# Stick-breaking attention: masking by a product on TensorE, or by a scan that restarts and a multiplication on GpSimd

## The chip, the cores and the metric

The kernel runs on one core of one Trainium2 chip. The time is the device time of one execution in microseconds, the median of three runs. One launch computes the whole model; everything happens on one core, so that one slow stage shows in the time directly.

The core's engines: TensorE (PE in the profile, PEld its weight loads), VectorE (DVE), ScalarE (ACT), GpSimd (POOL), and SyncE (SP), which here only issues the DMAs.

## The reference, cut to what matters

The model has 512 tokens of width 1024 and runs a first block (chunked attention and convolution), then two layers with an MLP each. The mixer of the last layer is "stick-breaking" attention with 8 heads of 128. That part is what the change touches:

```python
def blk_fn(args):
    i, qb = args
    z = jnp.einsum('bthd,bshd->bhts', qb, k).astype(jnp.float32) * d_h ** -0.5
    t_pos = i * SB_QBLOCK + jnp.arange(SB_QBLOCK)
    mask = key_pos[None, :] < t_pos[:, None]
    lo = jnp.where(mask, jax.nn.log_sigmoid(-z), 0.0)
    rc = lax.cumsum(lo, axis=3, reverse=True)
    log_a = jax.nn.log_sigmoid(z) + (rc - lo)
    a = jnp.where(mask, jnp.exp(log_a), 0.0)
    return jnp.einsum('bhts,bshd->bthd', a.astype(v.dtype), v)
```

For each query the softplus of the scores is summed from the last valid key backwards; a weight is exp(score minus that sum). A key counts only if it stands before the query, so in each diagonal block of 128 x 128 only the strict lower triangle is valid.

## The kernel before, in words

The program of each engine is written out by hand, with semaphores between them; nothing reorders it. Activations stand with channels on the partitions. A weight tile of 1024 x 256 (`raw`, 1 MB) is loaded by SP, rounded by ACT (`split`, line 1068, `wh<-raw`), and the rest is taken by DVE (`split`, line 1724, `wl<-raw,wh`, 128 x 2048); PE then makes three products per block (lines 451 to 453).

The last mixer is the stage `stick`: four groups of two heads (`attention_group`, g = 0 to 3), numbered 12 to 19, and a fifth call that only finishes heads 18 and 19 beside the first part of the output projection. In group g PE projects the six blocks of its own two heads (q, k, q, k, and values twice) and, between them, works off the two heads of the group before. Its program in groups 1 to 3 is: scores of the even head (`do_scores(0)`); blocks 0 and 1; the sum of squares of block 0 (`head_stat`); transposes of the even head's weights (`do_turns(0)`, line 555); block 2; `head_stat`; the product with the values of the even head (line 891); scores of the odd head; block 3; `head_stat`; block 4; transposes of the odd head (`do_turns(1)`); block 5; `head_stat`; the values' product of the odd head.

Scores of one head are a lower triangle by row blocks of 128 queries: 128, 256, 384 and 512 columns, in three PSUM banks. Behind each score product stands a second one, of an identity with a 128 x 128 mask of 0 and -1e30, which is added onto the diagonal block (lines 538 and 541).

The weights then come about in two halves (`HALVES`): the row blocks 0 to 2 (768 columns), and row block 3 (512 columns). ACT makes the softplus (`softplus`, lines 1380, 1383, 1384), DVE adds max(score, 0) (line 2263), scans backwards (line 2268, `suffix`, once per row block; the factor of the scan is `extra`, all ones), and subtracts the scan from the score in PSUM (line 2273), ACT takes the exponential (line 1393) and raises `a_ready`. The scan starts at the last column of a row block. A masked score of -1e30 has a softplus of 0 and a weight of exp(-1e30) = 0, so the masked columns change nothing.

PE's transposes are 10 blocks of 128 x 128: the first three wait for the first half (and for the PSUM banks, which DVE's line 2273 frees), the fourth for the second half. So one head's weights go round ACT, DVE, ACT before PE may go on, and PE stands still if they are late.

On DVE the odd head's last line 2273 is followed at once by `split(st, 2)`, one instruction of line 1724. GpSimd squares the q and k blocks for the norm (line 1693, and the low part, line 1698), and in the finishing call it splits one tile (line 1708); it has nothing to do with the weights. On ACT the exponentials stand in a fixed place between the evacuations of blocks.

Of the kernel before, what the change touches and what calls it, by code (L numbers as in the profile page):

```python
# [20 lines left out]
P = 128  # L21
# [104 lines left out]
def build(nc, xT, wst, par_d, wg_d, rb_d, small_d, mask_d, tab_d, tok_d, gain_d, out):  # L126
    with ExitStack() as ctx:
        def sb(name, shape, dt=F):
            return ctx.enter_context(nc.sbuf_tensor(name, shape, dt))
# [26 lines left out]
        ones_r = sb("ones_r", [P, P], R)  # L156
        ident_r = sb("ident_r", [P, P], R)
        mask_r = sb("mask_r", [P, P], R)
        SbB = sb("SbB", [P, 1280])
# [54 lines left out]
        g_log, g_scan, g_exp, g_prod, g_silu = (sem(n) for n in ("g_log", "g_scan", "g_exp", "g_prod", "g_silu"))  # L214
        sp_log, a_ready = sem("sp_log"), sem("a_ready")
        ob_lo = sem("ob_lo")
# [152 lines left out]
        def _(sp):  # L369
# [47 lines left out]
            ready(sp, ("gout", 1, 1))  # L417
            sp.dma_start(small[:, C_SN:C_SN + P], mask_d).then_inc(tables_in, 16)
            with sp.Fori(GLA_END, N_TILES // 2) as i:
# [8 lines left out]
        def _(pe):  # L428
# [101 lines left out]
            def scores(hd, q, k, rows):  # L530


                before = hd >= 12
                for b in range(3):
                    take(("score", hd, b))
                for t in range(NT):
                    w, b = (t + 1) * P, MIX[side(hd)][CBANK[t]]
                    last = mm(ps[b][:, COFF[t]:COFF[t] + w], q[rows, t * P:(t + 1) * P],  # L538
                              k[rows, 0:w], start=True, stop=not before)
                    if before:  # L540
                        last = mm(ps[b][:, COFF[t] + t * P:COFF[t] + w], ident_r[:], mask_r[:],
                                  start=False, stop=True)
                    if t:
                        last.then_inc(done[b], 1)
# [512 lines left out]
        def _(act):  # L1057
# [300 lines left out]
            def attention_group(name, g, hd, prev, qk0, soft):  # L1358
# [27 lines left out]
                def exponential(hh, *halves):  # L1386

                    if not soft:
                        for banks in halves or HALVES:
                            b, lo, w = banks[-1]  # L1390
                            settled(act, ("score", hh, b))
                            x = MIX_Sb[side(hh)][:, banks[0][1]:lo + w]
                            A(x, x, ACT.Exp).then_inc(a_ready, 1)

# [161 lines left out]
        def _(pool):  # L1556
# [130 lines left out]
            mlp("ffn0", 0, 4)  # L1687

            for n in range(16):
                st, q = Step("stick", n // 4), SQ[("qk", 8 + n)]  # L1690
                whole, (hi, lo) = sq[:, q % 2, :], sq_parts[n % 2]
                stands(pool, st, n % 4)
                g.tensor_tensor(whole, tmp[:, n % 2, :], tmp[:, n % 2, :], ALU.mult).then_inc(sq_whole, 1)
                pool.wait_ge(sq_whole, n + 1)
                pool.wait_ge(sq_ready, q + 1)
                if n >= 2:
                    pool.wait_ge(sq_used, STAT[("qk", 8 + n)] - 1)
                g.tensor_tensor(lo, whole, hi.bitcast(F), ALU.subtract).then_inc(sq_low, 1)


            so_ = Step("outc", 0)
            s = so_.slot(1)
            for a, ready_ in enumerate((third_hi, w_hi)):
                pool.wait_ge(ready_, so_.tile(1) + 1 if a else 1)
                if a:
                    pool.wait_ge(w_lo, so_.tile(1))
                for c in range(a * KC // 2, (a + 1) * KC // 2):
                    ins = g.tensor_tensor(wl[s][:, c, :], raw[s][:, c, :], wh[s][:, c, :].bitcast(F), ALU.subtract)
                ins.then_inc(w_lo if a else third_lo, 1)
            out_squares("outc", 5)  # L1710
            mlp("ffn1", 32, None)
# [3 lines left out]
        def _(dve):  # L1715
# [483 lines left out]
            def attention_group(name, g, hd, prev, qk0, soft):  # L2199
# [42 lines left out]
                def weights(hh, whole=True, last=None):  # L2242
# [17 lines left out]
                    for n, banks in enumerate(HALVES):  # L2260
# [5 lines left out]
                        for t in (3,) if n else (0, 1, 2):  # L2266
                            back = slice(OFF[t], OFF[t] + (t + 1) * P)
                            last = v.tensor_tensor_scan(suffix[:, back][:, ::-1], extra[:, 0:(t + 1) * P],  # L2268
                                                        Sb[:, back][:, ::-1], 0.0, ALU.mult, ALU.add)
# [84 lines left out]
            def mlp(name, hid0, key, n):  # L2354
# [22 lines left out]
                if not hid0:  # L2377
                    dve.wait_ge(tables_in, 48)
                    step(v.tensor_copy(ident_r[:], ident))
                    step(v.tensor_copy(ones_r[:], ones[:]))  # L2380
                    v.tensor_copy(mask_r[:], small[:, C_SN:C_SN + P]).then_inc(masks_set, 1)
                with dve.Fori(1, 3) as i:
# [3 lines left out]
            mlp("ffn0", 0, ("norm", 3), 4)  # L2386
            step(v.memset(extra[:, 0:S], 1.0))
            for g in range(4):
# [86 lines left out]
def constants():  # L2475
# [7 lines left out]
    small[:, C_GM:C_GM + P] = (i <= j) & (i // CH == j // CH)  # L2483
    earlier = np.where(j < i, 0.0, NEG).astype(np.float32)
    sign = np.where(np.arange(32) < 16, -1.0, 1.0).astype(np.float32)
    tok = np.stack([ca[0:32].T, sa[0:32].T * sign]).reshape(2, NT, P, 32)
    return small, earlier, np.stack([ci, si]), np.ascontiguousarray(tok.transpose(2, 0, 1, 3).reshape(P, -1))

# [22 lines left out]
```

## Time and profile before

| | us |
|---|---|
| median of 3 runs | 1630.54 (1629.6 to 1631.69) |
| the profiled execution, its own time | 1630.96 |
| its span, first to last instruction | 1629.2 |
| PE busy in the span | 1609.8 (99%) |
| DVE busy | 871.6 (53%) |
| ACT busy | 606.8 (37%) |
| POOL busy | 299.4 (18%) |
| granted TensorE clock, mean | 0.999 |

The profiled execution lies 0.4 us above the median, and 1.8 us of its time lie outside the span. A matmul's end is modelled and overlaps with the next one's start, so that the time a matmul takes from PE is read from start to start. A figure in square brackets at the end of a timeline row is the idle time of the engine before the instruction, with what ended it.

### The profile page before, as it was taken

The numbers are of one execution on the slowest core, as the hardware profiler recorded it, in microseconds if no ns is written. First come the engines' busy times: TensorE is split into PE (matmuls) and PEld (weight loads), VectorE is DVE, ScalarE is ACT, GpSimd is POOL, SyncE is SP. The second block draws the span as 40 slices with busy tenths as digits, with TensorE's granted clock in tenths as the row PEclk, the third lists the DMA queues.
The fourth block names the chain that finished last, engine by engine and source line by source line (L and its number), as shares of the span: only waits on it lengthen the run. The fifth ranks groups of instructions, "written<-read, shape, count | busy, mean of one in ns | idle before, by whom it ended". The sixth has DMA issues, their size and how long they took to land.

```text
span 1629.2 us, 20586 instructions
## 1 busy us (share of the span) xinstructions
PE 1609.8 (99%) x7870; PEld 1327.8 (81%) x7870; DVE 871.6 (53%) x1180; ACT 606.8 (37%) x842; POOL 299.4 (18%) x323
## 2 busy tenths in 40 slices
PE   8999999999999999999999999999999999999999
PEld 8888787887778988888888888888887888888887
DVE  7334564665779965453434434567766443434342
ACT  6323433234245555422222223466775422222121
POOL 0001110014245343210101012322122210101010
PEclk9999999999999999999999999999999999999999
DMA  6232222323211211222233223222211322223223
GB/s 213 104 103 78 77 77 78 99 95 103 78 52 53 84 54 56 99 104 95 87 103 103 93 87 104 78 78 78 74 57 52 103 104 96 90 99 103 103 78 104
DMA packets 24775, 145.66 MB, mean 89 GB/s; under 512 B 3824, under 2 KB 5248, under 8 KB 8064
## 3 DMA queue, kind: packets, MB, share of 16 engines
q1 hardware_dynamic: 24704, 144.67, 25.9%
q8 instruction: 49, 0.80, 0.2%
q14 instruction: 22, 0.18, 0.0%
HBM read 142.56 MB, written 2.10 MB: 89 GB/s over the span
## 4 chain that ended last, share of the span: by engine, by line
PE 88%; DVE 8%; ACT 2%; issue 1%; DMA 0%; SPq 0%; POOL 0%; DVEq 0%; ACTq 0%; POOLq 0%
PE ps_G L451 26%; PE ps_G L453 26%; PE ps_G L452 26%; PE ps_C L538 1%; PE ps_AV L891 1%; DVE wide L2089 1%; DVE top L2085 1%; DVE wl L1724 1%; PE ps_C L555 1%; DVE wide L2268 1%; PE ps_C L646 1%; PE ps_AV L673 1%; PE ps_C L742 1%; PE ps_C L891 1%; DMA h<-xT 0%
## 5 line engine op out<-in xcount | busy, mean ns | idle before, releaser
L451 PE MATMUL ps_G<-nh,wh 128*128 128x512 f32 x1032 | 404.5, 392 | 0.4 <-DVE h L1991 0.2
L453 PE MATMUL ps_G<-nh,wl 128*128 128x512 f32 x1032 | 401.7, 389 | 0.0
L452 PE MATMUL ps_G<-nl,wh 128*128 128x512 f32 x1032 | 401.6, 389 | 0.0
L1068 ACT ACTIVATE wh<-raw 128x2048 fp32r<-128x2048 f32 x127 | 242.4, 1909 | 327.3 <-PE ps_G L453 310.2
L1724 DVE TENSOR_TENSOR wl<-raw,wh 128x2048 fp32r<-128x2048 f32 x113 | 261.0, 2310 | 133.2 <-ACT wh L1068 128.5
L451 PE MATMUL ps_G<-ch,wh 128*128 128x512 f32 x816 | 323.3, 396 | 0.0
L453 PE MATMUL ps_G<-ch,wl 128*128 128x512 f32 x816 | 317.8, 389 | 0.0
L452 PE MATMUL ps_G<-cl,wh 128*128 128x512 f32 x816 | 317.7, 389 | 0.0
L451 PEld LDWEIGHTS ps_G<-nh,wh 128*128 128x128 f32 x1032 | 193.7, 188 | 46.0 <-issue 5.5
L453 PEld LDWEIGHTS ps_G<-nh,wl 128*128 128x128 f32 x1032 | 193.7, 188 | 40.5
L452 PEld LDWEIGHTS ps_G<-nl,wh 128*128 128x128 f32 x1032 | 193.8, 188 | 40.2 <-issue 0.5
L451 PEld LDWEIGHTS ps_G<-ch,wh 128*128 128x128 f32 x816 | 153.2, 188 | 39.1 <-issue 7.3
L452 PEld LDWEIGHTS ps_G<-cl,wh 128*128 128x128 f32 x816 | 153.3, 188 | 33.2 <-issue 2.2
L453 PEld LDWEIGHTS ps_G<-ch,wl 128*128 128x128 f32 x816 | 153.2, 188 | 32.2
L1676 POOL TENSOR_TENSOR tmp<-tmp 128x512 f32<-128x512 f32 x64 | 66.6, 1041 | 541.3 <-DVE tmp L2362 541.3
L2371 DVE TENSOR_TENSOR h<-h,ps_G 128x512 f32<-128x512 f32 x64 | 43.9, 687 | 167.6 <-PE ps_G L453 167.6
L1532 ACT ACTIVATE nh<-tmp 128x512 fp32r<-128x512 f32 x64 | 40.5, 632 | 248.4 <-DVE tmp L2362 248.4
L451 PE MATMUL ps_G<-wh,ch 128*128 128x256 f32 x384 | 111.2, 289 | 1.0 <-DVE tmp L2143 1.0
L452 PE MATMUL ps_G<-wl,ch 128*128 128x256 f32 x384 | 108.6, 283 | 0.0
L453 PE MATMUL ps_G<-wh,cl 128*128 128x256 f32 x384 | 108.6, 283 | 0.0
L2362 DVE SCALAR_TENSOR_TENSOR tmp<-ps_G,tmp 128x512 f32<-128x512 f32 x64 | 44.1, 689 | 91.5 <-PE ps_G L453 91.4
L1624 POOL TENSOR_TENSOR wl<-raw,wh 128x256 fp32r<-128x256 f32 x96 | 69.7, 763 | 85.3 <-ACT wh L1068 85.3
(369 smaller groups left out, 1773.1 us busy)
## 6 DMA issues: line engine op xcount, KB each, us to landing
raw<-wst SPq DMA_DIRECT2D x130, 1024.0 KB, 4.9
raw<-wst SPq DMA_DIRECT2D x4, 512.0 KB, 8.0
h<-xT SPq DMA_DIRECT2D x8, 256.0 KB, 7.7
outT<-h SPq DMA_DIRECT2D x8, 256.0 KB, 2.0
tabs<-rb_d SPq DMA_DIRECT2D x1, 1024.0 KB, 9.9
tabs<-tab_d SPq DMA_DIRECT2D x1, 512.0 KB, 3.8
small<-small_d SPq DMA_DIRECT2D x1, 192.0 KB, 9.3
SbB<-tok_d SPq DMA_DIRECT2D x1, 128.0 KB, 4.5
```

Source lines behind the costliest of these rows:

```text
L451: mm(o, ah, bh, start=first, stop=False)
L452: mm(o, ah, bl, start=False, stop=False)
L453: return mm(o, al, bh, start=False, stop=last)
L538: last = mm(ps[b][:, COFF[t]:COFF[t] + w], q[rows, t * P:(t + 1) * P], k[rows, 0:w], start=True, stop=not before)
L891: last = mm(bank_of(("av", hh))[:, j * P:S], vbuf[:, j, x * P:(x + 1) * P], MIX_PT[side(hh)][:, TOFF[j]:TOFF[j] + (NT - j) * P], start=j = ...
L1068: A(wh[s][:], raw[s][:], ACT.Copy).then_inc(w_hi, 1)
L1532: A(oh[:, k, :], tmp[:, k % 2, :], ACT.Square).then_inc(hid_hi, 1)
L1624: ins = g.tensor_tensor(wl[s][:, c, :], raw[s][:, c, :], wh[s][:, c, :].bitcast(F), ALU.subtract)
L1676: g.tensor_tensor(tmp[:, 2 + k % 2, :], tmp[:, k % 2, :], tmp[:, k % 2, :], ALU.mult).then_inc(hid_sq, 1)
L1724: v.tensor_tensor(wl[s][:], raw[s][:], wh[s][:].bitcast(F), ALU.subtract).then_inc(w_lo, 1)
L2362: moved_block(stt(out=tmp[:, k % 2, :], in0=ready_block(st, k), scalar=0.0, in1=tmp[:, 5, :], op0=ALU.max, op1=ALU.mult), st, k)
L2371: moved_block(tt(h[:, k - 8, :], h[:, k - 8, :], ready_block(st, k), ALU.add), st, k)
```

## The change: the mask moves from PE to the scan and to GpSimd

- The 32 mask products (line 541, four in each of eight heads) go, with the tiles of the identity and of the mask that they used.
- The scan's factor is no longer all ones. A second table, 128 x 512, has a zero in row p at column 512 - 128 - 1 + p, and ones elsewhere; it is read backwards over its last (t+1)*128 columns. The running sum is thus multiplied by zero at the last valid key of each query and starts anew there. The table comes by one more DMA on SP into `extra`, which replaces a memset of DVE.
- Masked columns now hold some other number after the exponential. GpSimd multiplies each diagonal block by a 128 x 128 table of ones and zeros, in place (`only_earlier`): three blocks behind the first half's exponential, one behind the second's. ACT raises a new semaphore `a_exp`, and GpSimd raises `a_ready`, for which PE waits.

```diff
@@ SP
-            sp.dma_start(small[:, C_SN:C_SN + P], mask_d).then_inc(tables_in, 16)
+            sp.dma_start(small[:, C_SN:C_SN + P], mask_d[:, 0:P]).then_inc(tables_in, 16)
+            sp.dma_start(extra[:, 0:S], mask_d[:, P:P + S]).then_inc(tables_in, 16)
@@ PE, scores
-                              k[rows, 0:w], start=True, stop=not before)
-                    if before:
-                        last = mm(ps[b][:, COFF[t] + t * P:COFF[t] + w], ident_r[:], mask_r[:],
-                                  start=False, stop=True)
+                              k[rows, 0:w], start=True, stop=True)
@@ ACT, exponential
-                            A(x, x, ACT.Exp).then_inc(a_ready, 1)
+                            A(x, x, ACT.Exp).then_inc(a_exp, 1)
@@ POOL
+            def only_earlier(hh):
+
+                for n in range(2):
+                    pool.wait_ge(a_exp, 2 * (hh - 12) + n + 1)
+                    for t in (3,) if n else (0, 1, 2):
+                        x = MIX_Sb[side(hh)][:, OFF[t] + t * P:OFF[t] + (t + 1) * P]
+                        ins = g.tensor_tensor(x, x, small[:, C_SN:C_SN + P], ALU.mult)
+                    ins.then_inc(a_ready, 1)
+
             for n in range(16):
+                if n > 4 and n % 4 == 1:
+                    only_earlier(10 + n // 2)
                 st, q = Step("stick", n // 4), SQ[("qk", 8 + n)]
...
                 g.tensor_tensor(lo, whole, hi.bitcast(F), ALU.subtract).then_inc(sq_low, 1)
+                if n > 4 and n % 4 == 3:
+                    only_earlier(10 + n // 2)
...
                 ins.then_inc(w_lo if a else third_lo, 1)
+                only_earlier(18 + a)
@@ DVE, scan
-                            last = v.tensor_tensor_scan(suffix[:, back][:, ::-1], extra[:, 0:(t + 1) * P],
+                            last = v.tensor_tensor_scan(suffix[:, back][:, ::-1], extra[:, S - (t + 1) * P:S][:, ::-1],
                                                         Sb[:, back][:, ::-1], 0.0, ALU.mult, ALU.add)
@@ DVE, end of the first MLP
-                    dve.wait_ge(tables_in, 48)
-                    step(v.tensor_copy(ident_r[:], ident))
-                    step(v.tensor_copy(ones_r[:], ones[:]))
-                    v.tensor_copy(mask_r[:], small[:, C_SN:C_SN + P]).then_inc(masks_set, 1)
+                    v.tensor_copy(ones_r[:], ones[:]).then_inc(masks_set, 1)
@@ DVE, before the stage
-            step(v.memset(extra[:, 0:S], 1.0))
+            dve.wait_ge(tables_in, 64)
@@ tables
-    earlier = np.where(j < i, 0.0, NEG).astype(np.float32)
+    earlier = (j < i).astype(np.float32)
+    reset = np.ones((P, S), np.float32)
+    reset[np.arange(P), S - P - 1 + np.arange(P)] = 0.0
```

The scores of an odd head as PE's program has them before, between the last values' product of the even head (`ps_AV<-PT,wide`) and block 3 (`ps_G`); `ps_C<-wide` is a score product:

```order
L891 MATMUL ps_AV<-PT,wide 128x128
L538 MATMUL ps_C<-wide 128x128
L541 MATMUL ps_C<-mask_r,ident_r 128x128
L538 MATMUL ps_C<-wide 128x256
L541 MATMUL ps_C<-mask_r,ident_r 128x128
L538 MATMUL ps_C<-wide 128x384
L541 MATMUL ps_C<-mask_r,ident_r 128x128
L538 MATMUL ps_C<-wide 128x512
L541 MATMUL ps_C<-mask_r,ident_r 128x128
L451 MATMUL ps_G<-ch,wh 128x512
```

and the same place in the changed program, where line numbers are a little different:

```order
L886 MATMUL ps_AV<-PT,wide 128x128
L536 MATMUL ps_C<-wide 128x128
L536 MATMUL ps_C<-wide 128x256
L536 MATMUL ps_C<-wide 128x384
L536 MATMUL ps_C<-wide 128x512
L450 MATMUL ps_G<-ch,wh 128x512
```

Four products of eight are gone; nothing else of PE's program moves.

GpSimd's program in group 1 before: squares and low parts of the blocks 0 to 3 (`sq<-tmp`, `nl<-sq,nh`), and then those of group 2:

```order
L1693 TENSOR_TENSOR sq<-tmp 128x512 [waits moved_G0]
L1698 TENSOR_TENSOR nl<-sq,nh 128x512 [waits sq_used,sq_ready,sq_whole]
L1693 TENSOR_TENSOR sq<-tmp 128x512 [waits moved_G1]
L1698 TENSOR_TENSOR nl<-sq,nh 128x512 [waits sq_used,sq_ready,sq_whole]
L1693 TENSOR_TENSOR sq<-tmp 128x512 [waits moved_G0]
L1698 TENSOR_TENSOR nl<-sq,nh 128x512 [waits sq_used,sq_ready,sq_whole]
```

and in the changed program, from block 0 of group 1 to its block 2, with the masking of the even head 12 (`Sb<-Sb,small`) between blocks 0 and 1:

```order
L1699 TENSOR_TENSOR sq<-tmp 128x512 [waits moved_G0]
L1704 TENSOR_TENSOR nl<-sq,nh 128x512 [waits sq_used,sq_ready,sq_whole]
L1690 TENSOR_TENSOR Sb<-Sb,small 128x128 [waits a_exp]
L1690 TENSOR_TENSOR Sb<-Sb,small 128x128 x2
L1690 TENSOR_TENSOR Sb<-Sb,small 128x128 [waits a_exp]
L1699 TENSOR_TENSOR sq<-tmp 128x512 [waits moved_G1]
L1704 TENSOR_TENSOR nl<-sq,nh 128x512 [waits sq_used,sq_ready,sq_whole]
L1699 TENSOR_TENSOR sq<-tmp 128x512 [waits moved_G0]
L1704 TENSOR_TENSOR nl<-sq,nh 128x512 [waits sq_used,sq_ready,sq_whole]
```

The odd head's four multiplications stand in the same way behind block 3. DVE's program at the end of an odd head is the same in both but for the line numbers; in the changed one it is:

```order
L2277 SCALAR_TENSOR_TENSOR wide<-extra,Sb 128x512 [waits dve_step]
L2282 TENSOR_TENSOR Sb<-ps_C,wide 128x512 [waits dve_step]
L1733 TENSOR_TENSOR wl<-raw,wh 128x2048 [waits w_hi,moved_C2]
L1777 SCALAR_TENSOR_TENSOR tmp<-ps_ST,wide 128x512 [waits sq_used]
L1767 SCALAR_TENSOR_TENSOR tmp<-tmp 128x512 [waits st_y]
```

(the scan is printed there as a SCALAR_TENSOR_TENSOR). The exponential of the second half, and so the fourth multiplication, can start only when line 2282 has ended, which is also when the split starts.

## Rows read from the trace of the kernel before

**Rows 1.** Windows, one group: us, busy (x) of PE, PEld, DVE, ACT, POOL, PEclk, DMA

```profile
1121.37:1168.31 46.94, 46.94 (x262) 39.52 (x261) 34.94 (x47) 33.12 (x52) 10.28 (x8) 1.00 0.20 68
```

**Rows 2.** Timeline (start, length, engine, line, operation), PE: scores of heads 9 and 15

```profile
608.30 2.32 PE L538 MATMUL ps_C<-wide 128*128 128x128 f32 x8
610.06 0.68 PE L451 MATMUL ps_G<-wh,ch 128*128 128x256 f32 x1
...
1146.93 0.39 PE L538 MATMUL ps_C<-wide 128*128 128x128 f32 x2
...
1149.49 0.45 PE L451 MATMUL ps_G<-ch,wh 128*128 128x512 f32 x1
```

**Rows 3.** Timeline of all engines: how head 14 (even, group 2) gets its weights

```profile
1121.80 0.69 DVE L1768 SCALAR_TENSOR_TENSOR tmp<-ps_ST,wide 128x512 f32<-128x512 f32 x1 [1.36 <-PE ps_ST L517]
...
1137.17 0.63 ACT L1393 ACTIVATE Sb<-Sb 128x512 f32<-128x512 f32 x1 [1.98 <-DVE Sb L2273]
...
1137.73 1.25 PE L555 MATMUL ps_C<-small,Sb 128*128 128x128 f32 x10
```

**Rows 4.** Timeline of all engines: head 15 (odd, group 2), to the group's end

```profile
1146.10 0.68 DVE L1768 SCALAR_TENSOR_TENSOR tmp<-ps_ST,wide 128x512 f32<-128x512 f32 x1
...
1157.06 1.29 POOL L1698 TENSOR_TENSOR nl<-sq,nh 128x512 fp32r<-128x512 f32 x1
1157.15 2.28 DVE L2268 TENSOR_TENSOR_SCAN wide<-extra,Sb 128x512 f32<-128x512 f32 x1
1158.24 0.83 ACT L1393 ACTIVATE Sb<-Sb 128x768 f32<-128x768 f32 x1
...
1160.20 0.63 ACT L1393 ACTIVATE Sb<-Sb 128x512 f32<-128x512 f32 x1 [1.13 <-DVE Sb L2273]
1160.20 2.29 DVE L1724 TENSOR_TENSOR wl<-raw,wh 128x2048 fp32r<-128x2048 f32 x1
1161.23 1.25 PE L555 MATMUL ps_C<-small,Sb 128*128 128x128 f32 x10
...
1168.31 0.40 PE L517 MATMUL ps_ST<-nl,ones_r 128*128 128x512 f32 x1
```

**Rows 5.** Timeline, DVE and POOL beside each other, and each alone

```profile
1091.57 1.04 POOL L1693 TENSOR_TENSOR sq<-tmp 128x512 f32<-128x512 f32 x1 [3.03 <-ACT tmp L1076]
...
1097.09 2.29 DVE L1724 TENSOR_TENSOR wl<-raw,wh 128x2048 fp32r<-128x2048 f32 x1 [0.79 <-ACT wh L1068]
...
1098.31 1.97 POOL L1693 TENSOR_TENSOR sq<-tmp 128x512 f32<-128x512 f32 x1 [4.32 <-ACT tmp L1076]
...
1227.79 1.22 DVE L2268 TENSOR_TENSOR_SCAN wide<-extra,Sb 128x512 f32<-128x512 f32 x1
```

**Rows 6.** Groups by line and shape, POOL's 128 x 128 operations: busy, mean ns

```profile
L1585 POOL TENSOR_SCALAR Sb<-Sb,cols 128x128 f32<-128x128 f32 x7 | 2.6, 375 | 169.5 <-DVE cols L1800 169.5
...
L1654 POOL TENSOR_TENSOR SbB<-SbB 128x128 f32<-128x128 f32 x2 | 0.9, 462 | 0.0
```

**Rows 7.** Timeline of all engines: the end of heads 18 and 19

```profile
1223.18 0.46 PE L538 MATMUL ps_ST<-wide 128*128 128x128 f32 x2 [0.72 <-DVE nl L2281]
...
1237.11 0.63 ACT L1393 ACTIVATE SbB<-SbB 128x512 f32<-128x512 f32 x1 [1.86 <-DVE SbB L2273]
1237.34 0.79 PE L555 MATMUL ps_ST<-small,SbB 128*128 128x128 f32 x4 [0.40 <-DVE SbB L2273]
```

**Rows 8.** Windows behind PE's longest idle time, columns as in rows 1

```profile
583.00:587.00 4.00, 3.99 (x9) 2.43 (x10) 3.86 (x10) 3.15 (x5) 0.77 (x2) 0.57 0.01 4
```

**Rows 9.** Timeline of PE: two idle times and what runs behind them

```profile
567.01 0.41 PE L879 MATMUL ps_ST<-small,tmp 128*128 128x128 f32 x2 [1.01 <-DVE tmp L2239]
...
583.01 4.09 PE L538 MATMUL ps_C<-wide 128*128 128x128 f32 x8 [3.42 <-ACT wide L1429]
```

**Rows 10.** Timeline: SP's DMA of the mask; DVE's split behind the memset of `extra`

```profile
541.10 0.33 SPq L418 DMA_DIRECT2D small<-mask_d  x1
...
1041.87 2.29 DVE L1724 TENSOR_TENSOR wl<-raw,wh 128x2048 fp32r<-128x2048 f32 x1 [1.03 <-ACT wh L1068]
```

More of the change, by code:

```diff
@@ L156, in build @@
         ones_r = sb("ones_r", [P, P], R)
-        ident_r = sb("ident_r", [P, P], R)
-        mask_r = sb("mask_r", [P, P], R)
         SbB = sb("SbB", [P, 1280])
@@ L214, in build @@
         g_log, g_scan, g_exp, g_prod, g_silu = (sem(n) for n in ("g_log", "g_scan", "g_exp", "g_prod", "g_silu"))
-        sp_log, a_ready = sem("sp_log"), sem("a_ready")
+        sp_log, a_exp, a_ready = sem("sp_log"), sem("a_exp"), sem("a_ready")
         ob_lo = sem("ob_lo")
@@ L530, in scores @@
             def scores(hd, q, k, rows):
-                before = hd >= 12
                 for b in range(3):
@@ L2483, in constants @@
     small[:, C_GM:C_GM + P] = (i <= j) & (i // CH == j // CH)
-    earlier = np.where(j < i, 0.0, NEG).astype(np.float32)
+    earlier = (j < i).astype(np.float32)
+    reset = np.ones((P, S), np.float32)
+    reset[np.arange(P), S - P - 1 + np.arange(P)] = 0.0
     sign = np.where(np.arange(32) < 16, -1.0, 1.0).astype(np.float32)
     tok = np.stack([ca[0:32].T, sa[0:32].T * sign]).reshape(2, NT, P, 32)
-    return small, earlier, np.stack([ci, si]), np.ascontiguousarray(tok.transpose(2, 0, 1, 3).reshape(P, -1))
+    return small, np.concatenate([earlier, reset], 1), np.stack([ci, si]), np.ascontiguousarray(tok.transpose(2, 0, 1, 3).reshape(P, -1))
 def kernel(**inputs):
```

## The prediction, made before the changed kernel was run

> **What bounds the kernel now.** I read the page first: PE is busy 99% of the span, and in its chain of waits PE holds 88%. The window of one group of the stage [rows 1] says the same: PE is busy 46.94 of 46.94 us, from the end of one group's last sum of squares (1121.37) to that of the next (1168.31), DVE 34.94, ACT 33.12, POOL 10.28. So at first sight whatever leaves PE is gained in full. I then read the timeline around the two places where PE takes over weights, because a busy share of 100% tells nothing of how near the others are to making it wait.
>
> In the even head's case [rows 3] the work starts behind PE: DVE's line 1768 at 1121.80 had waited 1.36 us for PE's last sum of squares. From there ACT and DVE go on by themselves; only the raw scores come from PE, in time. The second half's exponential ends at 1137.17 + 0.63 = 1137.80. PE starts its ten transposes at 1137.73, in steps of (1.25 - 0.27) / 9 = 0.109 us (0.27 being one transpose's own length), so the fourth, the first that needs this half, starts at 1137.73 + 3 x 0.109 = 1138.06. PE was 0.26 us away from waiting.
>
> In the odd head's case [rows 4] DVE's line 1768 at 1146.10 shows no idle time before it, so it had waited for DVE itself and not for PE. The weights' chain of the odd head thus hangs on the same start, 1121.37, through ACT and DVE, and not on when PE passes the even head. Its exponential ends at 1160.20 + 0.63 = 1160.83, and PE's fourth transpose starts at 1161.23 + 0.33 = 1161.56: 0.73 us to spare. What follows up to the group's end, 1168.31 - 1161.56 = 6.75 us, is PE's own. PE's clock is at its full level throughout [rows 1].
>
> **The change part by part.**
>
> Removed, 32 mask products. Four scores without masks take 610.06 - 608.30 = 1.76 us, with masks 1149.49 - 1146.93 = 2.56 us [rows 2], and the other heads of the stage show the same. That is 0.80 us a head, 6.4 us for eight, all of it on PE's path. But only so much of it counts as the weights' chain lets through: with 0.26 and 0.73 us to spare, a chain of unchanged length would leave PE at most 0.2 us at the even head and, since the odd head's limit stands relative to the same start, about 0.7 us per group in all.
>
> Added, four multiplications of 128 x 128 between each head's exponentials and PE. POOL's 128 x 128 operations take 0.46 us with two tensors and 0.38 us with a tensor and a column [rows 6]; I take 0.46. Now the wait of PE has a queue behind it: the fourth transpose, and with it blocks 2 or 5 and all later matmuls.
>
> Whether POOL may run at all is what decides. It and DVE hold each other up [rows 5]: line 1693 takes 1.04 us alone, but 1.97 us when it starts at 1098.31 inside line 1724's 1097.09 to 1099.38. It ends 0.90 us after DVE, so nearly the whole operation came behind (0.14 to 0.21 us of it are spared; rows 5 show 0.14, and I take 0.2 at most). The other way round [rows 4, 5]: the scan takes 1.22 us alone and 2.28 us when it starts at 1157.15 while POOL runs from 1157.06 to 1158.35. The one that started first runs out, the other waits.
>
> The Trainium skill, "SBUF — State Buffer", section "Who interferes with whom", gives the border of this: a DVE instruction with two SBUF inputs contends with a GpSimd instruction that reads SBUF, one with a single SBUF input does not. By it line 2273 and line 1768, which read PSUM and one SBUF tensor, let POOL through. No wait in the sum below is taken from either; if both blocked POOL, the even heads alone would be later, by some 0.4 us, which does not enter the sum.
>
> Even heads (14 as the pattern). The first three multiplications find POOL free and wait at most for the scan; they are done before the second exponential. The fourth runs from 1137.80 + 0.05 to 1138.31, and the fourth transpose starts at 1138.36, which is 0.30 us later than before, although PE arrived 0.80 us earlier. The 0.30 us does not add up: the odd head's chain does not see it.
>
> Odd heads (15 as the pattern). The first exponential ends at 1158.24 + 0.83 = 1159.07, the scan ends at 1157.15 + 2.28 = 1159.43. The three multiplications then run to about 1159.43 + 0.26 + 2 x 0.42 = 1160.53. DVE's split (line 1724, 2.29 us) wants to start at 1160.20, the same moment as the second exponential, because both are released by the same line 2273. It starts when the third multiplication is through, 1160.53, and ends at 1160.53 + 2.29 = 1162.82. The fourth multiplication is released at 1160.83 and finds the split running. It ends at 1162.82 + 0.26 = 1163.08, if it is spared 0.2 of its 0.46 us, and PE's fourth transpose starts at 1163.13. Before it was 1161.56: 1.57 us later. The rest of the group is PE's own, so the group is 1.57 us longer. There are three such groups (heads 13, 15, 17): 4.7 us. If the split gets in before the third multiplication, its end is 1162.49 plus some 0.1, and the third and the fourth come behind it: 1162.6 + 0.26 + 0.42 = 1163.28, and 1.8 us per group. I take the first.
>
> Finishing call. The scores of head 19 wait for DVE before and after (PE idle 0.72 us, to 1223.18 [rows 7]), so what head 18's scores save is lost there. The second exponential of head 19 ends at 1237.11 + 0.63 = 1237.74, and PE was already idle 0.40 us in front of its transposes (0.79 us for four of them, and a start at 1237.34): the fourth began near 1237.80. With a multiplication in between, and no split on DVE at this place, it starts at 1237.74 + 0.05 + 0.46 + 0.05 = 1238.30: 0.5 us later. Head 18's own delay is of the same kind and hides in front of the same chain.
>
> Small things, costed at nothing. The memset of `extra` goes; DVE stood idle for 1.03 us behind it, waiting for ACT [rows 10]. The two copies at the end of the first MLP stood on DVE in a stage bound by PE (PE 99% of the span). One DMA of 256 KB is added on SP behind the one at 541.10 [rows 10]; it delays tile loads there by no more than the issue of 0.33 us and a fraction of a 1 MB tile's time, and the DMA share in that slice of the page is 2 tenths. Without this cover it would be under 1 us. The scan reads its factor backwards and otherwise does the same work.
>
> The sum, against the profiled execution: 1630.96 + 4.7 + 0.5 = 1636.2. The runs' median lies 0.4 below that execution, so 1635.8 for the median; I write 1635.7.
>
> **Bounds.** The multiplication: 0.38 to 0.65 us (half way to line 1693's 1.04) moves each group by -0.1 to +0.2, and the third with it. With the split ahead of the third: +0.3 a group. If POOL could share with DVE: the fourth multiplication would end at 1160.83 + 0.05 + 0.46 = 1161.34 and the transpose start at 1161.39, 0.17 us earlier than before. So a group gives -0.2 to +2.1, the finishing call +0.3 to +0.7.
>
> **Rivals.**
>
> *A small multiplication gets through beside the split.* All blocked cases in the trace are of 128 x 512; a 128 x 128 block might find a gap, or the arbitration may favour it. Then three groups give 3 x -0.17 = -0.5, the finishing call +0.5: 1630.6, no change. For it speaks only that rows 5 do not show this size; against it, that line 1724 is one instruction of 2.29 us without a gap.
>
> *The saving comes through (the other side).* If the weights' chain got shorter with PE (because it waits for the raw scores somewhere) and POOL's part was hidden, each group would give 2 x 0.80 and the last call 0.80 or more: up to 6.4 us less, 1624.2; with half of it, 1627. For it speaks PE's 46.94 of 46.94 us. Against it, the 0.26 us at the even head and the 1.36 us that DVE waits for PE only at the start of the chain: the chain's length is ACT's and DVE's. It decides only if the exponentials end at least 0.7 us earlier relative to the group's start than now.
>
> *The clock falls.* PE would stand idle in front of the odd head's transposes from its arrival, about 1161.23 + 0.30 - 0.80 + 0.33 = 1161.06, to 1163.13, some 2 us, three times. An idle time of 1.01 us left the clock alone, one of 3.42 us was followed by a mean of 0.57 over 4 us [rows 8, 9], which is the lower of the two levels (1.2 GHz of 2.4) for most of them; the eight score matmuls behind it took 4.09 us against 2.32 us, 1.8 us more [rows 2, 9]. If 2 us were enough, three groups would lose 3 x 1.8 = 5.4 more: 1641.1. The 2 us lie nearer to 1.01 than to 3.42.
>
> **How the numbers follow.** The forecast (POOL blocked by the split, no change of clock) gets 0.70, with its own range of 1633.5 to 1638.0. POOL let through: 0.16. The saving comes through: 0.07. The clock falls: 0.07. A difference of 0.2%, 3.3 us, is about what a measurement can tell from none. Slower by more than that, above 1633.8: most of the forecast (0.67) and the clock's case (0.07), 0.74. Faster by more, below 1627.3: 0.06. The same: 0.20. The range for 8 in 10 takes in the forecast and most of the case without blocking: 1630.2 to 1638.5.
>
> **What would show it.** Right: the second multiplication group of heads 13, 15 and 17 (line 1690, one instruction) lasts about 2 us and ends 0.2 to 0.3 us behind DVE's split; PE shows an idle time of about 2 us at the fourth transpose there, released by POOL, and under 1.2 us in all at the even heads; the distance from one group's last sum of squares to the next is 48.5 us where it was 46.94; the scores take 1.76 us a head; the clock stays full. Wrong: that distance at or under 46.9, a multiplication of 0.5 us inside the split's time, or exponentials that end earlier against the group's start than 16.43 us (1137.80 - 1121.37) for the even and 39.46 us for the odd head.

## The result and the profile after

| | before | after |
|---|---|---|
| median, us | 1630.54 (11 runs, 1628.98 to 1631.69) | 1635.4 (11 runs, 1633.52 to 1636.2) |
| span of the profiled execution | 1629.2 | 1633.5 |
| granted TensorE clock, mean | 0.999 | 0.999 |

The changed kernel takes 1.0029 times as long, with an interval of 1.0021 to 1.0038: slower by 4.9 us between the medians, where 5.2 us were forecast (1635.7).

The window of group 2, the group of [rows 1], in the profile after, from the start of the second matmul of one group's last sum of squares to the same matmul of the next group; columns as in [rows 1]:

```profile
1121.78:1170.21 48.43, 46.66 (x254) 38.51 (x252) 35.06 (x47) 33.13 (x52) 16.52 (x16) 1.00 0.19 66
```

The group is longer, 48.43 us for 46.94, PE has 8 instructions fewer and 1.77 us without work, and POOL has 8 instructions more. The clock stays full.

Where the time sits is told by T, the start of the second matmul of a group's last sum of squares (line 517 before, 516 after), since ACT's and DVE's work of a group starts from it. From the timelines, in us:

| | T to T, group 1 | group 2 | group 3 | last T to the end |
|---|---|---|---|---|
| before | 45.48 | 46.94 | 46.94 | 413.93 |
| after | 47.12 | 48.43 | 48.41 | 414.83 |
| difference | +1.64 | +1.49 | +1.47 | +0.90 |

That is 5.5 us. The first T came 1.2 us earlier in the profile of after (1074.66 for 1075.89). Over all profiles of this study it lies between 1073.2 and 1076.4, and for the kernel before and the two kernels made from it alone between 1073.2 and 1075.9, so I put this part down to the single execution and not to the change. 5.5 - 1.2 gives the 4.3 us between the spans; the medians of 11 runs differ by 4.9.

The odd head of group 2, engine by engine, answers to [rows 4]:

```profile
1156.27 1.04 POOL L1699 TENSOR_TENSOR sq<-tmp 128x512 f32<-128x512 f32 x1 [7.41 <-ACT tmp L1071]
1157.39 1.30 POOL L1704 TENSOR_TENSOR nl<-sq,nh 128x512 fp32r<-128x512 f32 x1
1159.47 1.41 POOL L1690 TENSOR_TENSOR Sb<-Sb,small 128x128 f32<-128x128 f32 x3 [0.78 <-ACT Sb L1388]
1161.25 2.10 POOL L1690 TENSOR_TENSOR Sb<-Sb,small 128x128 f32<-128x128 f32 x1 [0.36 <-ACT Sb L1388]
```

```profile
1156.86 0.69 DVE L2272 SCALAR_TENSOR_TENSOR Sb<-ps_C,Sb 128x512 f32<-128x512 f32 x1
1157.59 2.19 DVE L2277 TENSOR_TENSOR_SCAN wide<-extra,Sb 128x512 f32<-128x512 f32 x1
1159.81 0.69 DVE L2282 TENSOR_TENSOR Sb<-ps_C,wide 128x512 f32<-128x512 f32 x1
1160.54 2.49 DVE L1733 TENSOR_TENSOR wl<-raw,wh 128x2048 fp32r<-128x2048 f32 x1
```

```profile
1161.55 0.49 PE L550 MATMUL ps_C<-small,Sb 128*128 128x128 f32 x3
1163.40 0.77 PE L550 MATMUL ps_C<-small,Sb 128*128 128x128 f32 x5 [1.35 <-POOL Sb L1690]
```

Read them together. DVE's split wants to start at 1160.54, finds POOL's third multiplication (it ends at 1160.88), and its record is 2.49 us long instead of 2.29: 0.20 us of it is waiting. POOL's fourth multiplication is released at 1161.25, falls into the split, takes 2.10 us instead of 0.46, and ends at 1163.35, 0.32 us behind the split's 1163.03. PE does three transposes and stands for 1.35 us. At the odd heads of groups 1 and 3 the same multiplication has records of 2.10 and 2.09 us, and PE waits 1.34 us.

The even head of the same group, all engines, answers to [rows 3]:

```profile
1135.49 1.34 DVE L2277 TENSOR_TENSOR_SCAN wide<-extra,Sb 128x512 f32<-128x512 f32 x1
...
1135.72 2.22 POOL L1690 TENSOR_TENSOR Sb<-Sb,small 128x128 f32<-128x128 f32 x3
...
1136.87 0.69 DVE L2282 TENSOR_TENSOR Sb<-ps_C,wide 128x512 f32<-128x512 f32 x1
...
1137.59 0.63 ACT L1388 ACTIVATE Sb<-Sb 128x512 f32<-128x512 f32 x1 [1.98 <-DVE Sb L2282]
...
1138.08 0.52 PE L550 MATMUL ps_C<-small,Sb 128*128 128x128 f32 x3 [0.20 <-POOL Sb L1690]
...
1138.30 0.46 POOL L1690 TENSOR_TENSOR Sb<-Sb,small 128x128 f32<-128x128 f32 x1 [0.37 <-ACT Sb L1388]
...
1138.81 0.98 PE L550 MATMUL ps_C<-small,Sb 128*128 128x128 f32 x7 [0.21 <-POOL Sb L1690]
```

No split stands here, and the fourth multiplication runs at once in 0.46 us. PE waits 0.41 us in two pieces. DVE's line 2282, which has one operand in PSUM, takes its usual 0.69 us though POOL's multiplications run beside it; the scan before it had held them up (2.22 us for three).

The finishing call, all engines, answers to [rows 7]:

```profile
1240.50 0.63 ACT L1388 ACTIVATE SbB<-SbB 128x512 f32<-128x512 f32 x1 [1.86 <-DVE SbB L2282]
1240.98 0.52 PE L550 MATMUL ps_ST<-small,SbB 128*128 128x128 f32 x3
1241.21 0.46 POOL L1690 TENSOR_TENSOR SbB<-SbB,small 128x128 f32<-128x128 f32 x1 [0.37 <-ACT SbB L1388]
...
1241.72 0.33 PE L550 MATMUL ps_ST<-small,SbB 128*128 128x128 f32 x1 [0.21 <-POOL SbB L1690]
```

The fourth transpose stands 23.10 us behind the last T, before 22.55: +0.55 us. What is left of the +0.90 us comes 10 us later, in DVE's part of the output projection, first after and then before:

```profile
1249.52 0.69 DVE L2000 TENSOR_TENSOR h<-h,ps_G 128x512 f32<-128x512 f32 x1 [1.05 <-PE ps_G L452]
1251.49 0.75 DVE L1798 SCALAR_TENSOR_TENSOR cl<-h,par,ch 128x512 fp32r<-128x512 f32 x1 [1.28 <-ACT ch L1101]
```

```profile
1245.60 0.69 DVE L1991 TENSOR_TENSOR h<-h,ps_G 128x512 f32<-128x512 f32 x1 [1.05 <-PE ps_G L453]
1247.22 0.75 DVE L1789 SCALAR_TENSOR_TENSOR cl<-h,par,ch 128x512 fp32r<-128x512 f32 x1 [0.93 <-ACT ch L1106]
```

The same instruction starts 1.28 us behind the end of the one before it instead of 0.93. ACT, for which it waits, works at the same distances in both: its line 1101 (1106 before) ends at 1251.03 and at 1247.10, 0.82 and 0.81 us behind the end of DVE's addition.

### The profile page after: what moved, and what is told of

Read it like the earlier page. It is cut to its first block, busy times and chain, and to the rows that moved or that the text cites. A ratio compares the mean times of both kernels' runs of the same rounds, so it can differ in the third digit from the quotient of the medians.

```text
span 1633.5 us, 20552 instructions
## 1 busy us (share of the span) xinstructions
PE 1607.2 (98%) x7838; PEld 1323.3 (81%) x7838; DVE 871.4 (53%) x1177; ACT 606.9 (37%) x842; POOL 323.3 (20%) x355
## 4 chain that ended last, share of the span: by engine, by line
PE 80%; DVE 14%; ACT 4%; issue 1%; POOL 1%; DMA 0%; SPq 0%; DVEq 0%; ACTq 0%; POOLq 0%
PE ps_G L450 24%; PE ps_G L452 24%; PE ps_G L451 24%; DVE wide L2277 2%; DVE wl L1733 2%; DVE wide L2098 1%; DVE top L2094 1%; DVE Sb L2282 1%; ACT wh L1063 1%; DVE Sb L2272 1%; DVE tmp L1768 1%; DVE tmp L1767 1%; ACT tmp L1086 1%; PE ps_C L641 1%; PE ps_AV L668 1%
## 5 line engine op out<-in xcount | busy, mean ns | idle before, releaser
L450 PEld LDWEIGHTS ps_G<-nh,wh 128*128 128x128 f32 x1032 | 193.7, 188 | 46.2 <-issue 5.1
```

The source lines that it names most:

```text
L450: mm(o, ah, bh, start=first, stop=False)
```

## The experiments

Theory after the result: a group is longer because POOL's fourth multiplication at the odd head is shut out by DVE's split. Open were two sizes (what the masks had cost PE, since PE arrived later than forecast) and whether the even head's wait adds up. Each of them was timed against the kernel before on the same chip (before: 1630.27 beside r1 to r4, 1630.5 beside r5 to r8, 1630.7 beside r9), with 5 runs for r1 and 11 for each of the others; the period is T to T in groups 2 and 3 of its profile.

| kernel | median, us | ratio to before, interval | period |
|---|---|---|---|
| r1_both_masks | 1636.29 | 1.0042, 1.0028 to 1.0055 | 48.75 |
| after | 1635.4 | 1.0029, 1.0021 to 1.0038 | 48.42 |
| r5_odd_only | 1634.28 | 1.0023, 1.0014 to 1.0032 | 47.89 |
| r8_masks_twice | 1632.42 | 1.0013, 1.0004 to 1.0022 | 47.87 |
| r7_before_weights_first | 1631.64 | 1.0008, 0.9999 to 1.0017 | 46.94 |
| r2_split_behind | 1631.05 | 1.0006, 0.9997 to 1.0015 | 46.88 |
| r4_even_only | 1630.68 | 1.0002, 0.9993 to 1.0011 | 46.87 |
| r6_weights_first | 1630.38 | 1.0000, 0.9991 to 1.0009 | 46.70 |
| r3_scan_from_high | 1629.72 | 0.9994, 0.9985 to 1.0003 | 46.31 |
| r9_split_halves | 1628.27 | 0.9984, 0.9975 to 0.9993 | 46.07 |

The differences of a few tenths of a us per group are read from the periods, which agree within 0.04 us between groups 2 and 3 of every kernel; the medians only say whether they reach the time.

**r2_split_behind: take the split away from the fourth multiplication.**

```diff
-                split(st, 2)
-                apply(2)
...
+                    def last_split():
+                        dve.wait_ge(a_ready, 2 * (prev + 1 - 12) + 2)
+                        split(st, 2)
+
+                    apply(2, last_split)
...
```

> The changed kernel with one DVE instruction moved: in groups 1 to 3 the last split of a group (128x2048) stands behind the mean of squares of block 2 and waits until GpSimd has done the odd head's fourth multiplication. Theory (the split locks GpSimd out): the multiplication takes 0.46 us instead of 2.10 and ends 0.54 us behind the exponential, PE's fourth transpose comes 1.6 us earlier against the group's start, three groups give 4.9 us: 1630.5, period 46.8. Rival (the multiplication is late because of GpSimd itself or its semaphores, and the split is a coincidence): no change, 1635.4.

Timelines of POOL, DVE and PE, same odd head:

```profile
1160.70 0.45 POOL L1690 TENSOR_TENSOR Sb<-Sb,small 128x128 f32<-128x128 f32 x1 [0.37 <-ACT Sb L1388]
```

```profile
1161.19 2.29 DVE L1733 TENSOR_TENSOR wl<-raw,wh 128x2048 fp32r<-128x2048 f32 x1 [0.50 <-POOL Sb L1690]
```

```profile
1161.02 1.25 PE L550 MATMUL ps_C<-small,Sb 128*128 128x128 f32 x10
```

The multiplication takes 0.45 us, PE's ten transposes run without a gap, and the period falls by 1.54 us to 46.88, where the theory said 46.8 and the rival no change. The time of 1631.05 is 0.5 us above the theory's. The split against the fourth multiplication is what makes the group longer.

**r1_both_masks: PE's mask products put back beside the multiplications.**

```diff
+                    if before:
+                        last = mm(ps[b][:, COFF[t] + t * P:COFF[t] + w], ident_r[:], mask_r[:],
+                                  start=False, stop=True)
...
+                    ts(mask_r[:], small[:, C_SN:C_SN + P], -1.0, 1e30, ALU.add, ALU.mult).then_inc(masks_set, 1)
```

> The changed kernel with the 32 mask products put back on PE, so that the masking is done twice (PE and GpSimd). Theory (PE stands in front of GpSimd's fourth multiplication anyway): the 0.80 us per head that PE gets back come off its idle time, the group period stays 48.4 us and the time 1635.4 within 0.5; PE's idle time at the fourth transpose of the odd heads falls from 1.35 us to about 0.6. Rival (the saving of 6.4 us was real and GpSimd's part costs 11): 1635.4 + 6.4 = 1641.8.

With 32 more products on PE the time is not 6 us longer, as the rival had it: they lie in front of the same wait. But it is not within the 0.5 us of the theory either: 1636.29, and the period is 48.75 for 48.42. The mask is taken from the new table, as (table - 1) x 1e30. PE waits 1.21 us at the odd head, where the theory left 0.6. POOL and DVE, same odd head:

```profile
1156.62 1.04 POOL L1705 TENSOR_TENSOR sq<-tmp 128x512 f32<-128x512 f32 x1 [7.90 <-ACT tmp L1077]
1157.74 2.09 POOL L1710 TENSOR_TENSOR nl<-sq,nh 128x512 fp32r<-128x512 f32 x1
1159.82 3.72 POOL L1696 TENSOR_TENSOR Sb<-Sb,small 128x128 f32<-128x128 f32 x4
```

```profile
1157.44 1.30 DVE L2283 TENSOR_TENSOR_SCAN wide<-extra,Sb 128x512 f32<-128x512 f32 x1
1158.78 0.69 DVE L2288 TENSOR_TENSOR Sb<-ps_C,wide 128x512 f32<-128x512 f32 x1
1159.50 2.49 DVE L1739 TENSOR_TENSOR wl<-raw,wh 128x2048 fp32r<-128x2048 f32 x1
```

Who waits has changed sides. POOL's work hangs on block 3, which is later here, so the scan starts first (1157.44) and is through in 1.30 us, and POOL's line 1710 waits (2.09 for 1.30). DVE reaches the split before POOL's first multiplication, and all four of them end behind it (1159.82 + 3.72 = 1163.54). The Trainium skill, "SBUF — State Buffer", section "Who interferes with whom", puts it as "Issue order, not op shape, decides who blocks". The traces agree: they have the same pair of instructions in both orders (scan 2.19 and POOL 1.30 after, scan 1.30 and POOL 2.09 here).

**r8_masks_twice: what a mask product costs.** The kernel before, with each mask product issued twice (so the added mask is -2e30).

```diff
-                        last = mm(ps[b][:, COFF[t] + t * P:COFF[t] + w], ident_r[:], mask_r[:],
-                                  start=False, stop=True)
+                        for again in range(2):
+                            last = mm(ps[b][:, COFF[t] + t * P:COFF[t] + w], ident_r[:], mask_r[:],
+                                      start=False, stop=again == 1)
```

> The kernel before with each of its 32 mask products issued twice. In its groups 1 to 3 PE waits for nobody after head 12, so the second set shows what one set costs PE. Theory after reading the traces (the first matmul behind unmasked scores holds PE 0.63 us instead of 0.28, so that a head's four mask products cost 0.45 us and not the 0.80 of the prediction): the two period-to-period distances of groups 2 and 3 grow from 46.94 to 47.8, the time by about 3: 1633.4. Rival (0.80 us per head as predicted): periods of 48.5, the time 1635.5.

Period 47.87: +0.93 us for the eight added products of a group, 0.465 us a head, not 0.80. (The time rose by 1.9 us and not by the 2.9 of the theory; in the profile group 1 is 0.45 us longer, groups 2 and 3 0.93 each, and the stretch behind the last T 0.1, which makes 2.4.) The cause of the difference stands in PE's timeline at the seam between the scores and block 3, after and before:

```profile
1147.71 2.32 PE L536 MATMUL ps_C<-wide 128*128 128x128 f32 x8
1149.47 0.80 PE L450 MATMUL ps_G<-ch,wh 128*128 128x512 f32 x1
1150.10 0.40 PE L451 MATMUL ps_G<-cl,wh 128*128 128x512 f32 x1
```

```profile
1149.49 0.45 PE L451 MATMUL ps_G<-ch,wh 128*128 128x512 f32 x1
1149.77 0.40 PE L452 MATMUL ps_G<-cl,wh 128*128 128x512 f32 x1
```

Behind bare scores the first matmul of the block holds PE for 1150.10 - 1149.47 = 0.63 us, behind a mask product for 0.28. From first score to second matmul of the block it is 2.39 us without masks and 2.84 with them (from 1146.93 in [rows 2]): 0.45 a head. Why bare scores let go of PE later was not tried.

**r3_scan_from_high: no masks on PE and no multiplications.** The scan starts at 1e30 instead of 0; the zero factor takes it to an exact 0 at the last valid key, and masked weights become exp(-1e30) = 0. PE waits for ACT again.

```diff
-                                                        Sb[:, back][:, ::-1], 0.0, ALU.mult, ALU.add)
+                                                        Sb[:, back][:, ::-1], 1e30, ALU.mult, ALU.add)
...
```

> The changed kernel without GpSimd's multiplications: the scan starts at 1e30 instead of 0, so that a masked column gets exp(score - 1e30) = 0 and the zero factor at the last valid key discards the 1e30. ACT releases PE again. Theory (without GpSimd the weights' chain on ACT and DVE is the limit, not PE): the odd head's fourth transpose comes 0.05 us behind its exponential, 39.4 us after the group's start, where it was 40.19 in the kernel before and 41.6 in the changed one; period 46.2, three groups 6.5 us and the last head 0.5 us less than the changed kernel: 1628.3. Rival (PE is the limit and the whole 6.4 us of the mask products come through): 1630.5 - 6.4 = 1624.1, period 45.3.

Time 1629.72, period 46.31, where the theory said 1628.3 and 46.2. Its reason was wrong: the odd head is not the limit. Its exponential ends 38.83 us behind T, 0.63 earlier than the 39.46 of before, and its fourth transpose starts 0.73 us later. What holds is the even head: exponential done at T + 16.43, fourth transpose at T + 16.49, where PE gets to it at T + 16.27 if nothing holds it (so in r9, below). Of 0.93 us saved per group 0.63 comes through.

**r4_even_only and r5_odd_only: the multiplications at even or at odd heads alone, the rest as r3.** The lines of r5; r4 has the other parity.

```diff
-                            A(x, x, ACT.Exp).then_inc(a_exp, 1)
+                            A(x, x, ACT.Exp).then_inc(a_exp if hh % 2 == 1 else a_ready, 1)
...
+                if hh % 2 != 1:
+                    return
...
```

> Scan from 1e30 as in r3, and GpSimd's four multiplications for the even heads 12, 14, 16 and 18 only. Theory (PE's delay at an even head does not add up, since the odd head's chain does not see it): as r3, 1628.3, though PE waits for GpSimd at every even head. Rival (each wait adds its own delay): 0.55 us for each of four even heads more than r3, 1630.5.

> Scan from 1e30, and GpSimd's four multiplications for the odd heads 13, 15, 17 and 19 only. Theory (the whole loss is made at the odd heads, by the split in front of the fourth multiplication; the even heads' wait hides in front of it): period 48.4 us as in the changed kernel, the time 1635.4. Rival (each head's wait adds): 0.55 us less for each of the four even heads, 1633.2 and a period of 47.9.

Even heads alone cost 0.56 us a group (46.31 to 46.87), odd heads alone 1.58 (to 47.89), together 2.11 (48.42): they add up, as the rival of both runs had it. In r4 PE waits at the even heads alone; its fourth transpose starts there at T + 17.03 for 16.49 in r3, and its odd transposes run without a gap. With multiplications at both heads the odd head's wait would hide this, if the even head's delay did not reach the odd head's weights. It does, by the scan of row block 3. DVE in r3 and in r4:

```profile
1156.93 1.66 DVE L2272 TENSOR_TENSOR_SCAN wide<-extra,Sb 128x512 f32<-128x512 f32 x1
```

```profile
1154.58 2.22 DVE L2279 TENSOR_TENSOR_SCAN wide<-extra,Sb 128x512 f32<-128x512 f32 x1
```

The odd head's exponential ends at T + 38.83 in r3 and at T + 39.41 in r4. DVE and PE in r5:

```profile
1158.01 1.67 DVE L2279 TENSOR_TENSOR_SCAN wide<-extra,Sb 128x512 f32<-128x512 f32 x1
...
1160.44 2.48 DVE L1735 TENSOR_TENSOR wl<-raw,wh 128x2048 fp32r<-128x2048 f32 x1
```

```profile
1163.29 0.98 PE L550 MATMUL ps_C<-small,Sb 128*128 128x128 f32 x7 [1.33 <-POOL Sb L1692]
```

The scan starts at the same distance from T as in the changed kernel, but takes 1.67 us instead of 2.19, because POOL's low part of block 3 ends 0.52 us earlier, as PE does block 3 that much earlier. With that the exponential ends at T + 38.86 instead of T + 39.39, and the fourth transpose starts at T + 41.08 instead of T + 41.62.

**r6_weights_first and r7_before_weights_first: DVE does the even head's weights ahead of the group's first split**, in r3 and in the kernel before.

```diff
+                if not soft and prev is not None:
+                    weights(prev)
                 if not soft:
                     split(st, 0)
...
```

> Scan from 1e30 without GpSimd (r3), and DVE works on the even head's weights before the first split of the group instead of behind it. Theory (in r3 the even head's second exponential holds PE's fourth transpose at 16.49 us into the group; DVE began that head's work 1.4 us late because of the split): the exponential ends 1 us or more earlier, PE does not wait for it any more, and the period is 46.94 - 2 x 0.45 = 46.0; group 1 gains about 0.8: 1.3 us less than r3, 1628.4. Rival (the wait moves: the split comes late and block 2 waits for its tile): PE idle in front of block 2, period at or over r3's 46.3.

> The kernel before with the same exchange on DVE. Theory (PE waits for nobody there except 0.4 us at head 12): groups 2 and 3 keep 46.94 us, group 1 gains 0.4 at most, the time 1630.1. Rival (a weights' chain that ends earlier is worth something even with the mask products): periods under 46.8.

PE in r6 at block 2 of group 2, and in r7 at the even transposes and block 2 of group 1:

```profile
1139.90 0.50 PE L450 MATMUL ps_G<-ch,wh 128*128 128x512 f32 x1 [0.37 <-DVE wl L1728]
```

```profile
1087.92 1.42 PE L555 MATMUL ps_C<-small,Sb 128*128 128x128 f32 x10 [0.29 <-DVE Sb L2273]
1090.01 0.50 PE L451 MATMUL ps_G<-ch,wh 128*128 128x512 f32 x1 [0.68 <-DVE wl L1724]
```

The weights are early, and now block 2 waits for the split that stands behind them. So the rival of r6 holds: its period is 46.70 where r3 had 46.31. In r7 groups 2 and 3 kept 46.94, as its theory said, but group 1 lost 0.89 us where a gain of up to 0.4 was expected.

**r9_split_halves: half of the split before the even weights, half behind, on top of r3.**

```diff
-                if not soft:
+                if not soft and prev is not None:
+                    split_part(st, 0, 0)
+                elif not soft:
                     split(st, 0)
...
                     weights(prev)
+                    if not soft:
+                        split_part(st, 0, 1)
```

> No GpSimd multiplications (the scan starts at 1e30 and the zero factor takes it to an exact zero), and VectorE's split of the query scores of block 0 in two halves by key chunks: one before the even head's weights, one behind them, so that the even head's weights start 1.15 us earlier and nothing long is put ahead of block 2. Theory: what holds the period of r3 at 46.31 is the even head's chain of weights alone (exponential done at T+16.43, fourth transpose at T+16.49, where TensorE would be at T+16.24); with it 1.15 us earlier TensorE never waits at an even head, the second half is ready before block 2, and the period is 46.94 - 2 x 0.465 = 46.0 us, time some 1.0 to 1.5 us under r3's 1629.7, about 1628.5. Rival: as in r6, the earlier scan falls behind a GpSimd instruction that it excludes, or block 2 or the odd head waits for a tile that is now late: a new idle of TensorE of 0.3 us or more in each group, period 46.3 or more, 1629.7 or more.

DVE and PE, even head of group 2, and the window of the group:

```profile
1133.90 1.83 DVE L2272 TENSOR_TENSOR_SCAN wide<-extra,Sb 128x512 f32<-128x512 f32 x1
1135.76 0.69 DVE L2277 TENSOR_TENSOR Sb<-ps_C,wide 128x512 f32<-128x512 f32 x1
1136.48 1.23 DVE L1734 TENSOR_TENSOR wl<-raw,wh 128x1024 fp32r<-128x1024 f32 x1
```

```profile
1137.20 1.25 PE L550 MATMUL ps_C<-small,Sb 128*128 128x128 f32 x10
```

```profile
1121.26:1167.33 46.07, 46.07 (x253) 38.63 (x252) 35.02 (x48) 33.21 (x52) 10.14 (x8) 1.00 0.20 69
```

The scan does fall behind POOL's line 1702 here (1.83 us), but there is room for it: no idle time is left at the even head, PE is busy 46.07 of 46.07 us, and the period is what the theory said, 46.94 - 0.93 = 46.01, within 0.06. The median is 1628.27 against 1630.7 for the kernel before in the same job. Of all versions tried, this is the one version whose interval against the kernel before leaves out 1 on the faster side, by 0.07 to 0.25%.

## Why the prediction was right, and where it was not

- **Who decides: right, and shown.** The forecast was that DVE's split shuts out POOL's fourth multiplication at three odd heads. The record of it is 2.10 us, ends 0.32 us behind the split (0.26 forecast), and r2 takes 1.54 us per group back, all of the 1.49 that the change had added, by moving the split alone. The third multiplication got in before the split, as chosen.
- **The size per group: 1.49 for 1.57.** Of it 1.43 lie up to the odd head's fourth transpose. The exponential's end was forecast at T + 16.43 and T + 39.46 and came at T + 16.44 and T + 39.39; the split started with it and lost 0.20 us instead of 0.33 to the third multiplication.
- **The masks: the mis-sized term.** "0.80 us a head" was the distance between the start of the scores and the start of the next matmul. That next matmul is 0.35 us slower to let go of PE behind bare scores, so the masks cost 0.45 to 0.465 us a head (r8). Largely for that PE reached the odd head's fourth transpose at T + 40.10 where T + 39.69 was assumed, 0.41 us later, and was held for 1.52 us where some 2 were forecast; the profile counts 1.35 us of it as idle, since it lets the third transpose's record run on. The sum did not feel it, since PE waited there anyway. It would have felt it in the rival where the saving comes through: the whole of it is 3.7 us and not 6.4.
- **"The 0.30 us does not add up" at the even head: the step that failed.** It does (r4, r5). The odd head's chain was taken to hang on T alone, but its last scan waits for POOL's low part of block 3, which hangs on PE through ACT. After has its even fourth transpose at T + 17.03, before at T + 16.69: +0.34. The odd scores then give 0.45 back, so block 3's sum of squares comes at T + 33.79 where before had it at T + 33.87, and the exponential too is within 0.07 us of before. The working let neither effect reach this chain; they have opposite signs and like sizes, and cancelled. That the exponential's distance from T stood still, on which the sum rests, was luck: without the even head's delay it is 38.86 (r5), and the group is 0.53 us shorter.
- **The finishing call: 0.55 for 0.5,** from one multiplication in front of PE; in r1 and r2, which have it too, the fourth transpose stands 23.08 and 23.09 us behind the last T. The further 0.35 us was not forecast. The longer pause in front of DVE's line 1798 is in the profiles of after, r3, r4, r5 and r6, and not in those of before, r1, r2, r7, r8 and r9. r3 and r6 have it without multiplications, and r1 and r2 have multiplications without it, so it is not the multiplications; what it is was not tried and stays open. So of the forecast 4.7 + 0.5 us the groups gave 4.6 and the last call 0.9, of which 0.35 has no explanation; that the sum came within 0.3 us of the median is in part luck.
- **The clock: right.** The idle time of 1.35 us left the window's clock at 1.00, its higher level, as the 1.01 us of [rows 9] had left it alone.
- **The rival of the small multiplication that gets through is refuted** by its 2.10 us. The rival of the saving is refuted for this change by the exponentials' ends, T + 16.44 and T + 39.39, where it wanted them 0.7 us earlier. Its idea that the chain waits somewhere for PE is partly right, though: in r3 the odd head's exponential ends 0.63 us earlier than before.
- **A bound with a slip.** "0.65 us (half way to line 1693's 1.04)" is not half way from 0.46, which is 0.75. Nothing hangs on it, since the multiplication took the 0.46 us of the sum.
- **The edit's saving exists but is small.** Without multiplications it is 0.63 us a group (r3), with room at the even head 0.87 (r9). The prediction's "about 0.7 us per group" for a chain of unchanged length is near r3's figure, but not for its reason, the odd head: what stops it is the even head's 0.2 us. The multiplications cost 2.11 a group against it.

## What to carry to other kernels

In this kernel an instruction put on GpSimd between a producer and the critical engine cost what was left of the DVE instruction it met and 0.3 us, not its own length. That held behind the split and the scan, which read two tensors in SBUF, and not beside DVE's line 2282, which reads one there and one in PSUM. So look first at what DVE starts in the moment that releases it, and hold that one back. To price work that leaves TensorE, measure up to the second instruction behind it, or double the work and look at the period; and when a chain is said to hang on one event, check each of its instructions that can be held up by the other engine for what that one waits for.

## What was not expected of the hardware

- The first 512-column matmul on rounded operands behind the bare f32 scores held PE for 0.63 us from start to start (after), 0.28 behind a mask product (before); its record is 0.80 us long for 0.45. A mask product of 128 columns so costs 0.116 us (0.93 / 8, r8), though 0.20 us (0.80 / 4) seem to vanish with it.
- A shift of a few tenths of a us changes which of DVE and POOL waits: the scan takes 1.30, 1.67 or 2.19 us at the same place in r1, r5 and after.
- The scan with the factor read backwards takes 1.22 us with nothing of POOL's in front of it (changed kernel, at 1238.52), as [rows 5] have it with all ones.
- The stage's first T lies within 3.2 us over the eleven profiles, one of each kernel, which is more than most of the differences tried here: periods tell them apart, a single span does not.
